# One VectorE subtraction for two neighbouring weight slots in the feed-forward stages of a two-layer encoder

## What is computed

```
def sq_relu_mlp(h, w1, w2):
    return jnp.square(jax.nn.relu(h @ w1)) @ w2
...
h = modulate(rmsnorm(x, W['norm_mlp_g'][l]), mod[:, 3], mod[:, 4])
x = x + mod[:, 5][:, None, :] * sq_relu_mlp(h, W['mlp_w1'][l], W['mlp_w2'][l])
```

## Time and profile before

| | |
|---|---|
| median of the runs shown | 3226.7 us (3221.82 to 3227.95) |
| span of the profiled execution, first to last instruction | 3222.3 us |
| PE busy | 3134.8 us |
| DVE busy | 2185.9 us |
| ACT busy | 1409.6 us |
| granted TensorE clock, mean | 0.995 |

### The profile page before, as it was taken

How to read it: one execution, slowest core, us unless ns; L and a number is a source line. 1 busy time by engine, 2 the same in 40 slices (tenths; PEclk the granted TensorE clock), 3 DMA queues, 4 the chain that set the end, 5 groups by cost and what they waited for, 6 DMA issues and landing times.

```text
span 3222.3 us, 80509 instructions
## 1 busy us (share of the span) xinstructions
PE 3134.8 (97%) x31624; PEld 2952.1 (92%) x31624; DVE 2185.9 (68%) x3943; ACT 1409.6 (44%) x2323; POOL 129.3 (4%) x245
## 2 busy tenths in 40 slices
PE   7999999998999999999999999999999999999998
PEld 3798888787999999999999988998999999999998
DVE  3676677776578978788788865455589954445445
ACT  2433436665354443333344654334464543343442
POOL 0000001110000000000000000000000000000000
PEclk9999999999999999999999999999999999999999
DMA  9887750002878888888777532432557754444443
GB/s 395 330 292 264 284 206 20 25 24 101 332 288 290 305 299 301 313 298 309 265 240 253 183 119 93 144 124 92 175 191 240 243 170 166 165 163 163 163 164 120
DMA packets 183225, 669.48 MB, mean 208 GB/s; under 512 B 21398, under 2 KB 21568, under 8 KB 182496
## 3 DMA queue, kind: packets, MB, share of 16 engines
q1 hardware_dynamic: 156096, 570.95, 49.3%
q0 software_dynamic: 26912, 95.47, 9.0%
HBM read 662.25 MB, written 4.09 MB: 207 GB/s over the span
## 4 chain that ended last, share of the span: by engine, by line
PE 90%; DMA 3%; DVE 3%; issue 1%; ACT 1%; SPq 1%; DVEq 0%; ACTq 0%; POOLq 0%
PE ps L2281 51%; PE ps L2264 8%; PE ps L2266 7%; PE ps L2265 7%; PE ps L2450 5%; DMA sb_raw<-stream 3%; PE ps L2226 1%; PE ps L2442 1%; PE ps L2215 1%; PE ps L2780 1%; PE ps L2781 1%; PE ps L2782 1%; PE ps L2824 1%; PE ps L2823 1%; PE ps L2394 1%
## 5 line engine op out<-in xcount | busy, mean ns | idle before, releaser
L764 ACT ACTIVATE sb_whi<-sb_raw 128x1024 fp32r<-128x1024 f32 x778 | 812.5, 1058 | 1124.8 <-PE ps L2281 703.8
L1252 DVE TENSOR_TENSOR sb_wlo<-sb_raw,sb_whi 128x1024 fp32r<-128x1024 f32 x778 | 942.7, 1223 | 410.8 <-ACT sb_whi L764 407.7
L2281 PE MATMUL ps<-sb_ah,sb_whi 128*128 128x288 f32 (+1 forms) x2776 | 487.0, 297 | 11.9 <-DVE sb_al L1601 8.2
L2281 PE MATMUL ps<-sb_al,sb_whi 128*128 128x288 f32 (+1 forms) x2776 | 484.4, 297 | 0.0
L2281 PE MATMUL ps<-sb_ah,sb_wlo 128*128 128x288 f32 (+1 forms) x2776 | 482.6, 296 | 0.0
L2281 PEld LDWEIGHTS ps<-sb_ah,sb_whi 128*128 128x128 f32 x2776 | 409.9, 189 | 16.9 <-issue 12.1
L2281 PEld LDWEIGHTS ps<-sb_al,sb_whi 128*128 128x128 f32 x2776 | 409.1, 189 | 0.0
L2281 PEld LDWEIGHTS ps<-sb_ah,sb_wlo 128*128 128x128 f32 x2776 | 408.6, 189 | 0.0
L2264 PE MATMUL ps<-sb_ah,sb_whi 128*128 128x288 f32 (+1 forms) x952 | 286.6, 301 | 2.0 <-DVE sb_x L1451 1.0
L2266 PE MATMUL ps<-sb_al,sb_whi 128*128 128x288 f32 (+1 forms) x952 | 283.1, 297 | 0.0
L2265 PE MATMUL ps<-sb_ah,sb_wlo 128*128 128x288 f32 (+1 forms) x952 | 282.5, 297 | 0.0
(11 more groups left out here) (350 smaller groups left out, 4665.0 us busy)
## 6 DMA issues: line engine op xcount, KB each, us to landing
sb_raw<-stream SPq DMA_DIRECT2D x1070, 512.0 KB, 4.6
sb_strip<-strips POOLq DMA_DIRECT2D x156, 512.0 KB, 5.3
sb_crow<-crow POOLq DMA_DIRECT2D x8, 512.0 KB, 5.9
sb_x<-xT SPq DMA_DIRECT2D x1, 2304.0 KB, 15.5
sb_x<-xT POOLq DMA_DIRECT2D x1, 2304.0 KB, 11.9
yT<-sb_x SPq DMA_DIRECT2D x4, 576.0 KB, 2.8
sb_lwa<-lw POOLq DMA_DIRECT2D x16, 130.0 KB, 2.5
sb_lwg<-lw POOLq DMA_DIRECT2D x16, 130.0 KB, 2.4
```

The costliest lines, as they stand in the source:

```text
L764: nc.scalar.activation(whi[:, q % SPL, :], raw[:, n, :], ACT.Copy).then_inc(hi_ready, 1)
L1252: nc.vector.tensor_tensor(wlo[:, q % SPL, :], raw[:, n, :], whi[:, q % SPL, :], ALU.subtract).then_inc(lo_ready, 1)
L2281: ins = mm(PS[:, m, 0:s.wide], w[:, n % SPL, a:a + P], z[:, 2 * p + j, 0:s.wide], start=False, stop=False)
```

## The change

```
@@ -1248,6 +1248,13 @@
             def split(s, j, it=0):
 
                 (n, _), q = place(s, j), s.q0 + j
+                if s.name[:2] in ("m1", "m2"):
+                    if j % 2:
+                        both = slice(n - 1, n + 1), slice(q % SPL - 1, q % SPL + 1)
+                        dve.wait_ge(hi_ready, it * s.per + (q + 1))
+                        nc.vector.tensor_tensor(wlo[:, both[1], :], raw[:, both[0], :], whi[:, both[1], :],
+                                                ALU.subtract).then_inc(lo_ready, 2)
+                    return
                 dve.wait_ge(hi_ready, it * s.per + (q + 1))
                 nc.vector.tensor_tensor(wlo[:, q % SPL, :], raw[:, n, :], whi[:, q % SPL, :],
                                         ALU.subtract).then_inc(lo_ready, 1)
```

## The result

The changed kernel takes 3338.42 us (median of four runs, 3335.97 to 3339.65); the kernel before, run beside it, takes 3225.38 us. The ratio is 1.0353, with a 95% interval of 1.0339 to 1.0367: 113 us slower, where 86 were forecast. The profiled execution spans 3337.2 us and took 3338.77.

What follows compares the result with a forecast made beforehand. PE's matmuls were taken as the bound, DVE counting only where PE waits for it. Terms of 32 + 16 + 18 + 12.5 + 8 = 86 us, added to 3226.7, gave 3313 us, with a range of 3293 to 3340.

Steps and rivals of the forecast that it cites:

- the clock: Rival: the clock falls to 0.50 behind all twenty gaps of 2 us and more, 28 us, 3341 us; chance 0.07.
- The pair: Joined DVE subtraction takes 2.29 us; 256 pairs give DVE back 18 us, costed at nothing because PE's matmuls cover it.
- Plain boundaries after m1 groups: At 16 boundaries (m1_0_3, m1_1_1 to m1_1_3), slot 0 waits for the pair: 2.0 us each, 32 us.
- Boundaries after m2 groups: At 19 boundaries without a burst, slot 0 comes late by 0.85 us on average with the restart: 16 us.
- Mixed boundaries: The burst of 1.91 us covers the pair ahead of slot 0: nothing lost, by 0.1 us.
- Third slots in layer 0: Behind 16 m1 groups, slot 2 waits for its pair behind two strips: 1.15 us each with restart, 18 us.
- m1_1_0 and into m2_1_0: Four wide boundaries with strips and no burst: stalls at slot 0 and third slot, 12.5 us after subtracting earlier waits.
- First groups: First groups of m1_0_0 and m1_1_0, pairs behind activations and a reciprocal: two stalls each, 8 us, the weakest term.
- The stream: Rival: late paired releases starve the weight transfers in 24 mixed groups, 48 us more, 3361 us; chance 0.07.
- The strips: Rival: the strips don't hold the third slot, so 18 and most of 12.5 us go, 3285 us; chance 0.04.
- faster: Rival: DVE's total work decides when PE goes on, so the 18 us count, 3209 us; chance 0.02.
- no change: Rival: PE finds slot 0's low part in time at plain boundaries too, 3227 us; chance 0.01.

Runs made afterwards that it cites:

- e9: Changed kernel with pairs ahead of the emptying of bank 0 and of the strips, but single instructions in m1_0_0, m1_1_0 and m2_1_0: 3222.3 us.
- e1: Changed kernel with pairs only on slots 2 to 7 of a group, single instructions for slots 0 and 1: 3270.9 us.
- e6: Changed kernel with slots 0 and 1 made ahead of emptying bank 0, and every pair at its even slot, ahead of the strips: 3239.6 us.
- e3: Changed kernel with each pair taken apart into two single instructions at the pair's place, each with its own wait and increment: 3266.1 us.
- e4: Changed kernel with high parts and pair of slots 0 and 1 ahead of the emptying of bank 0, on ACT and DVE: 3247.5 us.
- e8: Changed kernel with pairs only on slots (4,5) and (6,7), single instructions for slots 0 to 3: 3239.3 us.

## Why the prediction was right, and what it missed

The verdict and the mechanism held. The range held by 1.6 us (3338.4 under 3340), and only because its high end took in half of the clock's 28 us; the forecast itself was 25 us short. Two of the signs of being wrong that I had named did show: a clock of 0.50 behind the gaps, and waits at another slot than 0 and 2 (slot 6 in the first groups of m1_0_0 and m1_1_0, 1.72 and 1.73 us).

A wait costs more than the view lists. These are PE's first matmuls of slot 7 in m2_1_1, before and then in the changed kernel:

```profile
2742.94 0.29 PE L2264 MATMUL ps<-sb_bh,sb_whi 128*128 128x288 f32 x1
...
2768.42 0.29 PE L2264 MATMUL ps<-sb_bh,sb_whi 128*128 128x288 f32 x1
...
2825.90 0.29 PE L2271 MATMUL ps<-sb_bh,sb_whi 128*128 128x288 f32 x1
...
2852.47 0.29 PE L2271 MATMUL ps<-sb_bh,sb_whi 128*128 128x288 f32 x1
```

From slot 7 to slot 7 a group lasts 25.48 us before and 26.57 in the changed kernel, 1.09 more with a listed wait of 0.84; so I add 0.25 for each. With that the steps come out so:

- **The pair**: 2.29 us forecast, 2.288 measured. At nothing by itself: right (e9), and the time that DVE gets back (25 us busy, 18 forecast) is worth nothing, as said.
- **Plain boundaries after m1 groups**: 32 us forecast; 16 waits, together 34.1 listed, 35 with 0.25 each and 0.25 off at twelve for the wait for bank 3 that goes.
- **Boundaries after m2 groups**: 16 forecast; 19 waits, 13.1 listed, 17.8 us. The forecast for the two of the earlier trace rows, 0.95 and 0.70 with the restart left out, stands beside 0.84 to 0.87 (six waits) and 0.61 to 0.70 (twelve, as counted); one is 0.28.
- **Mixed boundaries**: nothing, by 0.1 us; 0.05 us each at six of them in m1_0_1 and m1_0_2. The margin that I had counted on wasn't there: the pair ends 1.76 us behind the beginning of the burst (1219.89 to 1221.65), not 1.69, and PE follows 0.13 behind it, not 0.05.
- **Third slots in layer 0**: 18 forecast; 15 waits, 15.3 listed, 19.0 us. That the strips hold them was right there; e1 and e6 showed that the later half's high part holds the same slot next.
- **m1_1_0 and into m2_1_0**: 12.5 forecast; eight waits, 12.5 listed, 14.5 with 0.25 each, less the 1.9 of before: 12.6.
- **First groups**: 8 forecast, the weakest term; five waits, 6.7 listed, 8.0.

These make 92.5 us where the sum had 86. Part of the 6 is a small term: between the end of a pair and PE's first matmul I had put 0.05 us; it is 0.13 to 0.14 ahead of slot 0 (2719.48 to 2719.62, 2829.96 to 2830.10) and 0.06 at a third slot (1229.74 to 1229.80). PE stands at one more wait ahead of slot 0, that for the bank; whether that makes the difference wasn't tried.

**The step that failed is the clock.** I had set the rival apart with 0.07, on one row: a gap of 2.47 us with no fall behind it. One such row says only that a gap need not bring the clock down. The row was luck: that place is ahead of the feed-forward parts, no kernel here edits it, and the wait is 2.46 to 2.48 us in all eleven profiled executions; five of them have a fall there, the changed kernel's among them:

```profile
467.37 0.80 PE L2288 MATMUL ps<-sb_ah,sb_whi 128*128 128x288 f32 x4 [2.47 <-DVE sb_wlo L1259]
...
468.61:472.02 3.41, 3.41 (x16) 3.41 (x15) 2.63 (x13) 0.00 (x0) 1.06 (x2) 0.50 0.17 49
```

In the feed-forward parts twelve of the changed kernel's 25 waits of 1.5 us and more brought the clock down, at 1.52 us each: 18 us. 92.5 + 18 = 110.5, and 110.6 was measured there. Nor is that sum a fit in one place: m1_1_0, from which neither 0.25 nor 1.52 was taken, has 13.1 us of listed waits, nine of them, and four falls; less the wait of 0.37 before, with its 0.25, that makes 20.8, and the stage is 20.8 us longer. The rival had every one of twenty long gaps fall, 28 us; the truth is a share of them, which neither the forecast nor the rival said. The remaining 4 us of the profiled span lie ahead of m1_0_0 and between the two parts.

Of the Trainium skill (TensorE: Matmul & The Clock Gate, HAM oscillation) the warning that gaps ahead of matmuls bring the clock down agrees with these twelve. Its example has waits of about 3 to 5 us, with a fall behind each; eleven of the twelve here are shorter, 1.7 to 2.5 us, and at that length it isn't each time, as 2717.44 to 2745.44 shows. The other place (Perfetto Trace Analysis, Optimizing Scalar/DVE Operations), that breaking instructions up lets work be done sooner where an unsaturated engine makes others wait, agrees with 2.18 us of wait with the pair and 0.66 with two singles in its place (e3).

**The other rivals.** The stream did not become the bound, though one sign that I had named for it did show: ACT's waits for transfers rose (us in total, times, longest us; before, then the changed kernel):

```profile
ACT sb_whi L764 <- DMA sb_raw<-stream: 234.1, 71, 11.3
...
ACT sb_whi L764 <- DMA sb_raw<-stream: 413.4, 138, 10.9
```

I had said that they would stay small. They are waits that nothing behind them feels: e4 releases in the same pairs, has 325.9 us of such waits, and loses nothing in the mixed groups from m1_0_1 to m2_0_2. The strips held the third slots as forecast; "faster" and "no change" fell with the first row of the waits.

## What to carry to other kernels

Joining two instructions of an engine that isn't the bound saves its fixed time (2.288 us here for two of 1.221) and moves the first result back to the second one's; ask for each place in the order what the first half stood ahead of, and how much work the consumer has until it needs it. If the pair is put ahead of what it would stand behind, it costs nothing where the engine has time for it (thirteen stages of e9), and still costs where the engine is full of other work or the later half comes late (e6, 11 us); where nobody waits for the engine, it also gains nothing. A wait put on TensorE must be priced with the falls of the clock that some of such waits bring, and one row without a fall doesn't settle that: look at the same place in several executions.

## What the runs showed of the hardware

Behind waits of equal length the granted clock falls at some and not at others. In the feed-forward parts of ten of these kernels (before, changed, e1 to e8) PE has 199 idle stretches of 0.25 to 1.5 us, none with a fall behind it; of 70 between 1.5 and 2.3 us, 29 have one, and all of 13 longer ones (up to 3.42). That is no rule for longer waits: ahead of these parts, at the place of 367.55 in the earlier trace rows, waits of 2.49 to 3.26 us have a fall in eight of the eleven executions, and at that of 469.51 waits of 2.46 to 2.48 in five. In the changed kernel the 2.18 us ahead of 2690.10 had a fall and the 2.18 ahead of 2719.62 none. In the feed-forward parts the fall begins between 0.6 us before and 1.6 us after PE goes on (0.59 after, at 2690.69) and lasts 3.41 us at 0.50; in a plain group it costs 1.52 us (29.52 against 28.00). What tells the waits with a fall from those without wasn't worked out here.
